# Where the attention weights are divided by their sums: six float32 products with a diagonal per unit, or GpSimd scaling and plain transposes

## The reference, cut to what matters

```python
q, k, v = ...                    # 6 query heads, 2 key/value heads, HEAD_DIM 64
scores = q @ k.T + bias          # per block of 128 queries, over 3 blocks of 128 keys
scores = where(valid, scores, -1e30)
m = maximum(max(scores), sink)
p = exp(scores - m)
p = p / (sum(p) + exp(sink - m))
out = p @ v
```

## Time and profile before

| | us |
|---|---|
| median of 3 timed runs | 2754.8 |
| lowest and highest of them | 2754.02, 2760.42 |
| span of the profiled execution | 2751.9 |

### The profile page before, as it was taken

One profiled execution on the slowest core, in us unless ns is written; L12 is line 12 of the kernel. 1 busy time (PEld: TensorE's weight loads), 2 busy tenths in 40 slices (PEclk: granted clock), 3 DMA queues, 4 the chain that ended last, 5 costly groups with the idle time before them and its releaser, 6 DMA issues.

```text
span 2751.9 us, 31627 instructions
## 1 busy us (share of the span) xinstructions
PE 2637.7 (96%) x12542; PEld 2080.4 (76%) x12542; DVE 1465.6 (53%) x1881; ACT 1029.3 (37%) x1600; POOL 1091.4 (40%) x605
## 2 busy tenths in 40 slices
PE   6889989999999999999999999999999999999997
PEld 2657757777888788877777788888788788888885
DVE  5646658797777722276766422433457655322225
ACT  4413655455444511345454321211354434312112
POOL 1322114256656544442211142322353655534443
PEclk8999999999999999999999999999999999999998
DMA  6453247321222343241123122111324233433322
GB/s 247 178 146 101 78 173 285 113 81 66 81 84 83 112 146 126 84 145 59 54 68 109 54 88 67 58 48 48 137 91 153 77 115 104 149 118 128 115 77 85
DMA packets 109619, 297.92 MB, mean 108 GB/s; under 512 B 13344, under 2 KB 28192, under 8 KB 109472
## 3 DMA queue, kind: packets, MB, share of 16 engines
q1 hardware_dynamic: 102592, 275.36, 29.4%
q10 hardware_dynamic: 3456, 10.73, 1.0%
q0 software_dynamic: 3424, 9.81, 0.9%
HBM read 233.09 MB, written 62.76 MB: 108 GB/s over the span
## 4 chain that ended last, share of the span: by engine, by line
PE 71%; DVE 5%; ACT 1%; issue 1%; POOL 1%; DMA 1%; POOLq 0%; SPq 0%; DVEq 0%; ACTq 0%
PE ps L1698 16%; PE ps L1700 15%; PE ps L1699 15%; PE ps L1732 5%; PE ps L1734 5%; PE ps L1733 5%; PE pc L1732 1%; PE pc L1734 1%; PE pc L1733 1%; PE pss L2026 1%; PE pc L2078 1%; PE pc L2080 1%; PE pc L2079 1%; POOL whl L3448 1%; DVE pad L2104 0%
## 5 line engine op out<-in xcount | busy, mean ns | idle before, releaser
L3448 POOL TENSOR_TENSOR whl<-wraw,whl 128x1024 fp32r<-128x1024 f32 (+2 forms) x309 | 648.0, 2102 | 1242.0 <-ACT whl L2918 1241.8
L1698 PE MATMUL ps<-act,whl 128*128 128x512 f32 x1824 | 735.5, 403 | 34.7 <-DVE act L2098 9.2
L1699 PE MATMUL ps<-act,whl 128*128 128x512 f32 x1824 | 718.0, 394 | 0.0
L1700 PE MATMUL ps<-act,whl 128*128 128x512 f32 x1824 | 717.5, 393 | 0.0
L1698 PEld LDWEIGHTS ps<-act,whl 128*128 128x128 f32 x1824 | 344.9, 189 | 134.9 <-issue 43.3
L2918 ACT ACTIVATE whl<-wraw 128x1024 fp32r<-128x1024 f32 (+2 forms) x309 | 268.1, 869 | 461.9 <-PE ps L1700 372.6
L1700 PEld LDWEIGHTS ps<-act,whl 128*128 128x128 f32 x1824 | 344.9, 189 | 76.9
L1699 PEld LDWEIGHTS ps<-act,whl 128*128 128x128 f32 x1824 | 345.3, 189 | 75.7 <-issue 4.1
L2098 DVE TENSOR_TENSOR y<-y,ps 128x512 f32<-128x512 f32 x176 | 120.9, 687 | 365.6 <-PE ps L1700 365.4
L1698 PE MATMUL ps<-hid,whl 128*128 128x512 f32 x544 | 216.8, 399 | 4.4 <-DVE y L2502 4.3
L1700 PE MATMUL ps<-hid,whl 128*128 128x512 f32 x544 | 214.4, 394 | 0.0
(11 more groups left out here) (402 smaller groups left out, 4206.1 us busy)
## 6 DMA issues: line engine op xcount, KB each, us to landing
wraw<-in_w_in SPq DMA_DIRECT2D x63, 512.0 KB, 3.4
wraw<-in_f1u SPq DMA_DIRECT2D x72, 256.0 KB, 2.8
wraw<-in_f2d SPq DMA_DIRECT2D x36, 512.0 KB, 3.4
wraw<-in_w_out SPq DMA_DIRECT2D x32, 512.0 KB, 3.4
x<-in_w_ada SPq DMA_DIRECT2D x32, 512.0 KB, 7.2
hid<-hscr SPq DMA_DIRECT2D x29, 512.0 KB, 6.6
xs<-y SPq DMA_DIRECT2D x24, 512.0 KB, 6.3
wraw<-in_f2u SPq DMA_DIRECT2D x48, 256.0 KB, 3.3
```

The costliest lines, as they stand in the source:

```text
L1698: pe.matmul(PSB[g.bank][:, :], hi, x_hi, start=e == 0, stop=False)
L1699: pe.matmul(PSB[g.bank][:, :], hi, x_lo, start=False, stop=False)
L1700: m = pe.matmul(PSB[g.bank][:, :], lo, x_hi, start=False, stop=e == len(ks) - 1)
L3448: return g_.tensor_tensor(out, a, b, op)
```

## The change

ACT no longer writes scaled diagonals: `att_diag` and its tiles `dg` are gone. In its place in the plan stands `att_scale`, and POOL has the code for it: two instructions a unit that multiply the weights in place by the reciprocal, one per head, 128x384 (128x256 at either end). TensorE's step `att_t` becomes a transpose with the identity, and waits for POOL (`attP`) where it waited for ACT. The loads of `dist` and `alt` are counted on one semaphore, so their readers wait for both. The tiles `pt` and `small` move up by the room of `dg`. The plan's estimate for `att_t` stays, and so does the order of all other steps.

```diff
@@ attention() in plan_kernel
             if 0 <= u - 2 < nu:
-                p.put("att_diag", u - 2)
+                p.put("att_scale", u - 2)
@@ tensor: att_t
-                    w.wait_ge(*done("attA", "diag", u, g))
+                    w.wait_ge(*done("attP", u, g))
...
-                        m = pe.matmul(PSB[tb][:, s * 128:s * 128 + 128], scb[u % 3][:, g, s * 128:s * 128 + 128],
-                                      dgs[u % 2][:, g, :], start=True, stop=True)
+                        m = pe.transpose(PSB[tb][:, s * 128:s * 128 + 128], scb[u % 3][:, g, s * 128:s * 128 + 128], ident[:, :])
@@ vector: att_score, tensor: fft_mid
-                w.wait_ge(*done("d_dist"))
+                w.wait_ge(*done("d_mix", "alt"))
@@ scalar
-            def att_diag(u):
-                w.wait_ge(*done("attD", "recip", u))
-                if u >= 2:
-                    w.wait_ge(*done("att", "t", u - 2, 1))
-                for g in range(2):
-                    av(dgs[u % 2][:, g, :], ident[:, :], ACT.Copy, scale=small[:, u % 3, 10 + g:11 + g]).then_inc(
-                        *mark("attA", "diag", u, g))
@@ gpsimd
+            def att_scale(u):
+                lo, hi = span(UNITS[u][1])
+                w.wait_ge(*done("attD", "recip", u))
+                for g in range(2):
+                    sc = scb[u % 3][:, g, 0:hi - lo]
+                    g_.tensor_scalar(sc, sc, small[:, u % 3, 10 + g:11 + g], None, ALU.mult).then_inc(*mark("attP", u, g))
```

More of the change, by code:

```diff
@@ L1293, in build @@
         scb.append(vT[:, 0:768].rearrange("p (g k) -> p g k", g=2))
-        dgs = [sb(f"dg{b}", [P, 2, 128], c=ca) for b in range(2)]
         pts = [sb(f"pt{b}", [P, 384], c=ca) for b in range(2)]
@@ L1949, in fft_mid @@
             def fft_mid():
-                w.wait_ge(*done("d_alt"))
+                w.wait_ge(*done("d_mix", "alt"))
                 w.wait_ge(*done("apD", "t", 0, 1, 7))
@@ L3430, in scalar @@
                      "ssm_out": ssm_out, "glu_gelu": glu_gelu, "glu": glu, "glu_out": glu_out, "att_v": att_v,
-                     "att_exp": att_exp, "att_diag": att_diag, "att_t": att_t, "att_out": att_out, "att_split": att_split, "fft_c": fft_c, "fft_split": fft_split,
+                     "att_exp": att_exp, "att_t": att_t, "att_out": att_out, "att_split": att_split, "fft_c": fft_c, "fft_split": fft_split,
                      "nadd": nadd, "r_fac": r_fac, "r_sq": r_sq, "r_fac2": r_fac2, "r_store": r_store,
@@ L3542, in gpsimd @@
             steps = {"yb_split": yb_split, "wb_split": wb_split, "split": split, "apply": apply, "tab_vst": tab_vst, "tab_wst": tab_wst, "tab_kst": tab_kst,
-                     "tab_cst": tab_cst, "ssm_rot": ssm_rot, "ssm_back": ssm_back, "glu_out": glu_out, "r_add": r_add,
+                     "tab_cst": tab_cst, "ssm_rot": ssm_rot, "ssm_back": ssm_back, "att_scale": att_scale, "glu_out": glu_out, "r_add": r_add,
                      "pair_low": pair_low, "hid_split": hid_split, "m_split": m_split}
@@ L3655, in mix_load @@
                 w.wait_ge(*done("apD", "t", 0, 1, 7))
-                q.dma_start(dist[:, :], t["dist"]).then_inc(*dmark("d_dist"))
-                q.dma_start(alt[:, :], t["alt"]).then_inc(*dmark("d_alt"))
+                q.dma_start(dist[:, :], t["dist"]).then_inc(*dmark("d_mix", "dist"))
+                q.dma_start(alt[:, :], t["alt"]).then_inc(*dmark("d_mix", "alt"))
             def u_store(i, t_):
```

## The result

| | us |
|---|---|
| median before, beside it on the same chip | 2756.9 |
| median after (2771.58 to 2777.97) | 2773.1 |
| ratio, with its 95% interval | 1.0059 (1.0046 to 1.0072) |
| span of the profiled execution of after | 2776.2 |

The change makes the kernel 16.3 us slower (0.0059 x 2757). I had forecast 2757 with a range up to 2768: the time lies outside, on the slow side. As a difference, I had forecast +2.5 us, from the median of 2754.8 of three timed runs; a fourth makes it 2756.9. The long waits are at the four places where the prediction put them.

The account below looks back on a forecast made before the run. TensorE was taken as the bound in mid-attention. Over four blocks, gains of 0.5 and 1.8 us and losses of 3.7 and 1.1 made 2.5 us slower: from 2754.8 to 2757 us, range 2746 to 2768.

Parts of the forecast that it names:

- What bounds the kernel: Mid-attention, 310 to 339 us: TensorE, busy all 29.00 us at full clock, is the bound; ACT is not.
- The rival in which the saving arrives whole: Attention: collisions rare, POOL scales while it would wait anyway, TensorE stays the bound; up to 2738 us, chance 0.10.
- What TensorE saves: All 132 attention products become transposes: some 16.9 us off TensorE; ACT loses 48 instructions, 18.8 us.
- What POOL adds: 48 scalings on POOL, each taken as 0.6 us, with a range of 0.4 to 1.0.
- First, POOL's order: Scalings queue behind rotations at t(4), t(10), t(17) and a split at t(12): score(13) 1.4 us late, score(20) 2.3.
- the sum by blocks: Four blocks of the model, cut at loads of `Cb`: gains 0.5 and 1.8 us, losses 3.7 and 1.1.
- Second, DVE beside POOL: POOL's scalings hold up DVE's two-input work behind reciprocals: 0.6 us a collision, two a block, later four.
- Third, the clock: TensorE's granted clock falls after the wait before t(10): 1.2 us charged there.
- POOL as the bound: Rival: scalings of 1.5 us make POOL the bound, 2770 us, slower from P = 1.1; chance 0.12.
- Transposes that don't hold the clock: Rival: from 320 to 343 us transposes let TensorE run at half clock for some 20 us: 2774 us, chance 0.05.
- Transposes of two records: Rival: a float32 transpose is two records too, TensorE saves nothing, link costs stay: about 2762 us, chance 0.03.
- What I had named as signs: Wrong if waits for POOL sum under 2 us, scaling exceeds 1 us, or clock stays low over 10 us of attention.

Follow-up runs that it names:

- e1: The changed kernel without POOL's scalings, transposes waiting for the reciprocal alone, the division left out: 2746.9 us, 0.9966 of the kernel before.
- e5: The changed kernel with POOL's scalings cut to the first 128 columns of each head: 2766.8 us, 1.0033 of the kernel before.
- e7: The kernel before plus 48 POOL scalings of the same shapes into a tile nobody reads, and the one semaphore for `dist` and `alt`: 2759.9 us, 1.0007.
- e11: The changed kernel with one two-input TENSOR_TENSOR a unit on POOL for both heads, in place of two scalings: 2775.4 us, 1.0067 of the kernel before.
- e13: The changed kernel with extra TensorE products of constants before the waits at t(4), t(10), t(12) and t(17): 2770.6 us, 1.0052 of the kernel before.
- e2: The kernel before with plain transposes instead of products, ACT still writing the diagonals, the division missing: 2750.3 us, 0.9977.
- e6: The changed kernel with float32 products by the identity in place of transposes, POOL's scaling kept: 2775.8 us, 1.0070 of the kernel before.

## Why the prediction was wrong

**What bounds the kernel**: half right. Windows with TensorE at 29.00 of 29.00 us did mean that it was the bound there, but not by much. e1 is the proof: only 9.4 of 16.9 us arrive, then DVE with its loads of `Cb` is the next in line. The rival in which the saving arrives whole, 2738, was out of reach in this plan, even with no scaling at all (2746.9).

**What TensorE saves**: right in kind and size. 132 records; six transposes take 0.87 us with their tail, and (0.87 - 0.273)/5 is 0.12 each, where I took 0.113 from the earlier trace rows. ACT lost 14.1 us, not 18.8: I multiplied the duration of one diagonal, 0.392, by 48, but successive ones overlap, and the view of before's ACT groups gives all 48 only 16.4 us of busy time.

**What POOL adds**: wrong, and the first step that failed. I took 0.6 us by halving the slope of two-input rows, because a scaling reads one tensor, and gave 1.0 as the upper end. It takes 1.25. From 0.61 us at 128 columns (e5), 0.92 at 256 (the shortest in the result's row) and 1.25 at 384, POOL needs 2.5 us per 1000 columns and 0.29 of its own: a multiply with a scalar from a tile is slower per column than one with two tensors (1.28 us at 512 columns). The argument "reads less, so takes less" had no row behind it. The nearest rows gave 1.01 (the line through 1.28 at 512 and 2.36 at 1024 columns starts at 0.20 us, not at 0.16, which gave me 0.97), and nothing made that an upper end. The Trainium skill, "GPSIMD Engine Reference", section 4.1, holds that work with one input is near line rate; the runs disagree by a factor of four to the 0.32 us estimated from it.

**First, POOL's order**: right in its four places, too small in size, about half of that as a result of the length. e5, with a scaling as long as I had assumed, is 9.1 us slower than before, not 2.5; so of the 13.8 us by which I missed, 7.2 are the length and 6.6 lie in other terms (each of the two to within some 5). The waits before t(4), t(10), t(12) and t(17) are 2.72, 3.19, 2.92 and 4.08 us.

e5 also tests the sum by blocks. I had -0.5, -1.8, +3.7 and +1.1; e5 shows -0.7, -1.0, +4.1 and +2.7. Three blocks of four stand within 0.8 us. That is closer than it deserves, since the terms inside are off in both directions (the collisions too dear, the waits too cheap), and its time of +9.1 is above the 5.2 of those blocks. With 1.25 us the blocks are 0.0, +1.5, +9.5, +6.3. My slope of 1.4 us for each 0.1 of the scaling, times 6.5, is 9.1; measured are 7.2 in time and 12.1 in the blocks. So with the right length the same sum would have said slower by 2.5 + 9.1 = 11.6. Some 5 us of 16.3 were missing still, and they lie in blocks 3 and 4, where delays feed each other. The third load of `Cb`, 1.5 us late, had brought the rotation before t(10) 1.6 us later (319.81 less 2.94, against 315.30), two scalings of 1.25 made score(13) 4.4 late, the split came 5.3 late (329.07), unit 12's scaling behind it took 1.3 more than I had, and score(15) was 9.7 late (339.34), where I had 1.6. That is the second step that failed: I reckoned each term against a rotation that started on the old time, and a split that was at most 0.9 us late (the scalings behind it end at 324.35 by the old times, at 325.2 in my sum), so the delay of one link did not carry into the next. And I put at nothing, without a reason, DVE's wait for POOL's `xt` behind the scalings: 2.8 us of waiting.

**Second, DVE beside POOL**: wrong. I charged some eleven collisions of 0.6 us, 6.8 in all, from one row in which POOL had two inputs. With one input it cost +1.9 (-1.1 to +5.0) in e7, the queue ahead of `xt` included, although the scalings were twice as long as in my charge. The row was real, but for another kind of instruction, as e11 shows. With one input it is mostly POOL that pays: the changed kernel's 48 scalings take 64.0 us, where 36 of 1.25 and 12 of 0.92 would be 56. The same holds in e5, where they average 0.78 us, not 0.61, so part of the 6.6 us above may lie here; no run tells how much.

**Third, the clock**: direction right, extent wrong, price about right. I charged 1.2 us at one place. The granted clock is 0.84 on average from 250 to 390 us, and four score products take 1.65 instead of 0.92 at 324.08. But e13 lifts it to 0.94 for 2 us, with an interval of some 5: most of the time lost to the slow clock looks like time in which TensorE would have waited anyway. The match of 2 with my 1.2 is in part luck, since I had one cold stretch and there are several.

**The rivals.** Of POOL as the bound the long scaling came, P = 1.25 against the 1.1 from which I had it count as slower: 0.12 was too small a chance for a duration that no row showed. POOL itself was not full (78.38 of 140 us); the chain through it binds. Transposes that don't hold the clock: refuted as the cause of the loss, by e1, 1.00 over 29 us with them in every round and a faster kernel. I had cited the Trainium skill, "TensorE: Matmul & The Clock Gate", Part 4, for it; in e1, with gemm and model products between the transposes, its rule did not show; whether it has a part in the 0.94 of e2 or in the higher clock of e6 than of after, and what it would do to transposes alone, no run here tells. Transposes of two records: refuted by their 132 records.

**What I had named as signs.** A scaling of over 1 us, and a granted clock that stays low over more than 10 us of the attention: both came true, the second with an average of 0.57 from 350 to 370 us. The third, waits for POOL of under 2 us in sum, did not: they were 21.1.

## What to carry to other kernels

A step that is moved to an idle engine joins that engine's list: its price is its own length there plus the wait of whatever stands ahead of it, and if that waits for a second chain, the move ties two chains together that ran apart. A delay then moves the steps ahead of the next link too, so reckon each term from the shifted times. Look for the length of that very instruction on that very engine, and if the trace hasn't it, let the nearest row stand as the middle of the range, not as its end. Before crediting a saving on a full engine, ask how far the next chain is behind: here 9.4 of 16.9 us.

## What the runs showed of the hardware

- **POOL, float32, 128 partitions.** A multiply by a scalar from a tile takes 0.61, 0.92 and 1.25 us at 128, 256 and 384 columns. A TENSOR_TENSOR of two heads at once with the reciprocal repeated takes 1.47 us at 768 columns undisturbed: 1.9 ns a column in all, against 3.3 for a scaling of 384. The same scaling of 384 columns takes 0.60 us on ACT and 0.42 on DVE.
- **Who gives way.** Beside POOL's one-input scalings DVE's two-input rows grow by about a tenth (`H<-Hb,xt` 682 ns before, 761 after, 755 in e7), while POOL's stretch, up to 2.2 us. Beside its two-input scalings DVE's grow by half (1034 ns in e11). The Trainium skill, "SBUF — State Buffer", section "Who interferes with whom", says that DVE's work with two inputs and GpSimd's work that reads SBUF block each other on a shared pair of ports, whoever starts first holding it; e11 fits that. The page makes no difference between one and two inputs on GpSimd, where these runs show a large one. Why one-input scalings are the ones to give way, no run here tells.
- **TensorE.** A float32 128x128 transpose is one record of 0.12 us in a row, a float32 product of that size two records and 0.24.
